# Norms in two groups of columns between grouped weight units of an f32 transformer kernel

## The reference

```python
def rmsnorm(x, g): return x * rsqrt(mean(x * x, axis=-1) + EPS) * g
h = rmsnorm(x, g) * (1 + scale) + shift        # per feature; scale, shift differ for image and context
x = x + gate * (mixer(h) @ w_out)
x = x + gate2 * feed_forward(rmsnorm(x, g2) * (1 + scale2) + shift2)
```

## Time and profile before

| what | value |
|---|---|
| runs | 3505.76, 3510.49, 3510.88 us; median 3510.49 |
| profiled execution | 3510.39 us, span 3509.1 us, mean granted clock 0.984 |
| TensorE busy | 3327.1 us, 95% of the span |
| VectorE busy | 1789.2 us, 51% |
| ScalarE busy | 1255.0 us, 36% |
| GpSimd busy | 233.9 us, 7% |
| DMA | 334.28 MB, mean 95 GB/s |

### The profile page before, as it was taken

The page is one execution under the profiler, slowest core; times in us unless marked ns, Lnnn a source line. Parts: engine busy times, 40 slices in busy tenths (PEclk is TensorE's granted clock), DMA queues, the critical chain, the costliest instruction groups (busy, mean ns, idle before and its releaser), DMA issues.

```text
span 3509.1 us, 43200 instructions
## 1 busy us (share of the span) xinstructions
PE 3327.1 (95%) x18016; PEld 2762.5 (79%) x18016; DVE 1789.2 (51%) x2728; ACT 1255.0 (36%) x1781; POOL 233.9 (7%) x319
## 2 busy tenths in 40 slices
PE   6998989999989999989999999989999989989998
PEld 4787778888877878767888786778888878668886
DVE  3678355333345445547666356366435434644343
ACT  4568342112234234244222435342212243543232
POOL 1001200000110000010001000100000110010001
PEclk9999999999999999999999999999999999999999
DMA  4500133323211211225544211133323221112222
GB/s 195 216 22 1 48 115 126 120 91 126 88 65 54 99 57 60 81 72 172 176 160 147 76 47 55 37 108 126 124 88 127 96 73 66 49 66 99 93 97 90
DMA packets 88643, 334.28 MB, mean 95 GB/s; under 512 B 11264, under 2 KB 14336, under 8 KB 84864
## 3 DMA queue, kind: packets, MB, share of 16 engines
q1 hardware_dynamic: 67280, 252.85, 20.5%
q0 software_dynamic: 21168, 78.65, 7.0%
HBM read 329.37 MB, written 2.10 MB: 94 GB/s over the span
## 4 chain that ended last, share of the span: by engine, by line
PE 90%; ACT 4%; DVE 4%; issue 1%; DMA 0%; POOL 0%; SPq 0%; ACTq 0%; DVEq 0%; POOLq 0%
PE PS L362 65%; PE PS L402 6%; PE PS L387 3%; PE PS L604 3%; PE PS L371 2%; PE PS L582 2%; PE PS L525 1%; PE PS L540 1%; PE PS L697 1%; PE PS L572 1%; PE PS L655 1%; PE PS L513 1%; PE PS L708 1%; ACT aPT L920 1%; ACT WH L768 1%
## 5 line engine op out<-in xcount | busy, mean ns | idle before, releaser
L768 ACT ACTIVATE WH<-WR 128x1024 fp32r<-128x1024 f32 (+1 forms) x376 | 418.8, 1114 | 1499.1 <-PE PS L362 1293.9
L362 PE MATMUL PS<-HH,WH 128*128 128x512 f32 x2912 | 879.9, 356 | 18.5 <-DVE WL L1162 10.0
L362 PE MATMUL PS<-HH,WL 128*128 128x512 f32 x2912 | 876.9, 355 | 0.0
L362 PE MATMUL PS<-HL,WH 128*128 128x512 f32 x2912 | 874.6, 355 | 0.0
L1162 DVE TENSOR_TENSOR WL<-WR,WH 128x1024 fp32r<-128x1024 f32 (+1 forms) x376 | 487.0, 1296 | 751.4 <-ACT WH L768 750.9
L362 PEld LDWEIGHTS PS<-HH,WH 128*128 128x128 f32 x2912 | 481.1, 188 | 109.4 <-issue 14.8
L362 PEld LDWEIGHTS PS<-HH,WL 128*128 128x128 f32 x2912 | 479.5, 188 | 79.6
L362 PEld LDWEIGHTS PS<-HL,WH 128*128 128x128 f32 x2912 | 478.5, 188 | 80.4 <-issue 1.0
L362 PE MATMUL PS<-DH,WL 128*128 128x512 f32 (+1 forms) x1056 | 318.7, 356 | 0.0
L362 PE MATMUL PS<-DH,WH 128*128 128x512 f32 (+1 forms) x1056 | 318.7, 356 | 0.0
L362 PE MATMUL PS<-DL,WH 128*128 128x512 f32 (+1 forms) x1056 | 318.7, 356 | 0.0
(11 more groups left out here) (272 smaller groups left out, 3994.1 us busy)
## 6 DMA issues: line engine op xcount, KB each, us to landing
WR<-in_win SPq DMA_DIRECT2D x176, 512.0 KB, 3.5
AT<-in_adat POOLq DMA_DIRECT2D x144, 512.0 KB, 3.8
WR<-in_wdn SPq DMA_DIRECT2D x64, 704.0 KB, 4.0
WR<-in_wret SPq DMA_DIRECT2D x64, 512.0 KB, 3.2
WR<-in_zin SPq DMA_DIRECT2D x36, 512.0 KB, 3.5
AR<-in_ada SPq DMA_DIRECT2D x8, 1024.0 KB, 11.5
aV<-in_ada SPq DMA_DIRECT2D x8, 1024.0 KB, 4.9
aAR<-in_ada SPq DMA_DIRECT2D x8, 1024.0 KB, 6.6
```

Source lines behind the costliest of these rows:

```text
L362: mm = PE.matmul(dst[:, a:b], w[u % 2][:, k * P:(k + 1) * P], h[:, k, a:b], start=(k == 0 and i == 0), stop=(k == nk - 1 and i == 2))
L768: AC.activation(M.WH[u % 2][:, 0:n], M.WR[u % 2][:, 0:n], COPY).then_inc(*on.up("w_hi", u))
```

## The change

The norms between stages (all but "0a") are made in two groups of columns. For "0b", "1a", "2b" and "3a" group 0 is the image and group 1 the context; for "2a" it is the other way round; for "1b", "3b" and "final" the groups are the two halves of the image. `product_tail` makes the last two units before a norm group by group: group 0 of both, then group 1 of both, with group 0's two mean matmuls inside the first unit's group 1. `product_groups` makes the first two units after it: group 0 in halves of four tiles, then group 1, with group 1's mean matmuls inside the first half. It stands in front of the feed-forwards and of the retention; in front of the mixers of layer 2 the row products go context first, and in front of those of layer 3 they need the image alone.

DVE's `norm` weaves the updates of X, the scaling, the low parts and the two refills of the next stage in one written order, ACT's `norm` does the same with squares, roots and high parts. The scale is now applied by DVE together with the root for every tile (not for tile 0 alone), so that ACT adds the shift and rounds to HH in one instruction; L810 and L814 are gone there. "2a" has no grouped tail: its context comes by DMA early, so its norm is made beside the last product of layer 1. The root, half and scaled tiles have buffers of their own (`NORM`). GpSimd's sums of the tail's tiles, the last norm's scaling and the 8 stores of 128 x 512 are split by group as well (16 stores of 128 x 256). SyncE's waits name group 1.

In the calls, `norm(tag, l, which, segs)` becomes `norm(tag, l, which, update, c)` with c the next stage's first unit, and `mean_square(tag, segs)` is gone but for the first norm. Cut to its core:

```diff
...
+def groups(tag):
+    if tag in ("1b", "3b", "final"):
+        return (0, L, 0), (L, S, 0)
+    return ALL if tag != "2a" else ALL[::-1]
+def tail_tiles(tag):
+    return {"1b": ((4, 5), (6, 7)), "2a": ((), (7,)), "0a": ((), ())}.get(tag, ((6,), (7,)))
+def tail_place(ps, tag, v, g):
+    a, b, _ = groups(tag)[g]
+    return ps[v][:, 512 * g:512 * g + b - a]
...
+    def product_groups(u, dst, tag, between):
+        for g, (a, b, _) in enumerate(groups(tag)):
+            for k0, k1 in ((0, KT // 2), (KT // 2, KT)) if g == 0 else ((0, KT),):
+                for v in range(2):
+                    if g == 0 and k0 == 0:
+                        PE.wait_ge(*on("w_lo", u + v))
+                    for k in range(k0, k1):
+                        between(g, v, k)
+                        if v == 0:
+                            PE.wait_ge(*on("h_lo", (tag, g, k)))
+                        for i, (w, h) in enumerate(((WH, HH), (WH, HL), (WL, HH))):
+                            mm = PE.matmul(dst[v][:, a:b], w[(u + v) % 2][:, k * P:(k + 1) * P], h[:, k, a:b],
+                                           start=(k == 0 and i == 0), stop=(k == KT - 1 and i == 2))
+                    if g == 1:
+                        mm.then_inc(*on.up("product", u + v))
+    def product_tail(u, src, nk, tag, after):
+        hi, lo = src
+        for g, (a, b, _) in enumerate(groups(tag)):
+            for v in range(2):
+                if g == 0:
+                    PE.wait_ge(*on("w_lo", u + v))
+                    PE.wait_ge(*on(*after[v]))
+                for k in range(nk):
+                    beside_tail(tag, g, v, k)
+                    for i, (w, h) in enumerate(((WH, hi), (WH, lo), (WL, hi))):
+                        mm = PE.matmul(tail_place(PS, tag, v, g), w[(u + v) % 2][:, k * P:(k + 1) * P], h[:, k, a:b],
+                                       start=(k == 0 and i == 0), stop=(k == nk - 1 and i == 2))
+                mm.then_inc(*(on.up("product", u + v) if g else on.up("tail", (tag, v))))
+    def mean_part(tag, g, i):
+        a, b, _ = groups(tag)[g]
+        PE.wait_ge(*(on("squared", piece(tag, KT - 1, g)) if i else on("square_summed", piece(tag, KT - 2, g))))
+        mm = PE.matmul(mean_place(PS, tag)[:, a:b], M.ONE[:, :], M.WK[(2, 1)[i]][:, a:b], start=(i == 0), stop=(i == 1))
+        if i == 1:
+            mm.then_inc(*on.up("mean_square", (tag, g)))
+    def beside_tail(tag, g, v, k):
+        if g == 1 and v == 0 and k in (2, 5):
+            mean_part(tag, 0, k // 5)
+    def beside_head(tag):
+        def between(g, v, k):
+            if g == 0 and v == 0 and k in (2, 3):
+                mean_part(tag, 1, k - 2)
+        return between
     def product_pair(u, dst, segs, ready, between=None):
...
                 product(up + 2 * j + 1, PS[1], (HH, HL), KT, segs, free[1])
-            for m in range(KT):
+            for m in range(KT if ch == 0 or l == 1 else KT - 2):
                 after = (None, ("up_taken", (l, (ch + 1) * FC - 1)), (gate, (l, (ch + 1) * FC - 1)))[m] if m < 3 else \
                     ("x_down", (l, ch, m - 2))
-                product(down + m, PS[m % 2 if m else 2], (M.DH, M.DL), FC, segs, after, ("d_lo", l, ch) if m == 0 else None)
+                product(down + m, PS[m % 2 if m else 2], (M.DH, M.DL), FC, segs, after, ("d_lo", l, ch) if m == 0 else None,
+                        context_mean if ch and m == KT - 1 else None)
+        if l != 1:
+            product_tail(down + KT - 2, (M.DH, M.DL), FC, {0: "1a", 2: "3a", 3: "final"}[l],
+                         [("x_down", (l, 1, m)) for m in (KT - 4, KT - 3)])
+    def context_mean(k):
+        if k == 7:
+            for i in range(2):
+                mean_part("2a", 0, i)
...
+        def image_mean(at):
+            if at in (4, 6):
+                mean_part(f"{l}a", 1, at // 6)
+        for g, tiles in enumerate((range(4, 6), range(4)) if l == 2 else (range(4),)):
+            for v in range(2):
+                product_rows(u + v, 4, 4 * v, L, tiles, place, v == 0, v == 1, ("h_lo", f"{l}a", g), True, None,
+                             image_mean if g == 0 and v == 0 else None, l == 3 or g == 1)
         mixed = [PS[3], PS[2]]
         for p in range(ROWS_AT):
             z = MIX[p]
+            if z == 12 and l == 3:
+                PE.wait_ge(*on("h_lo", ("3a", 1, KT - 1)))
             if p == MIXED_AT:
                 PE.wait_ge(*on("av_normed", l))
...
-    def norm(tag, l, which, segs):
-        n = segs[-1][1]
-        if tag == "0a":
-            AC.wait_ge(*on("step", ("scl", 0, 1)))
-        else:
...
-                for a, b, j in segs:
-                    i = AC.activation(HH[:, k, a:b], t[:, a:b], IDENT, bias=MOD[:, l, 24 * which + k, j:j + 1])
-            else:
-                for a, b, j in segs:
-                    i = AC.activation(t[:, a:b], t[:, a:b], IDENT, bias=MOD[:, l, 24 * which + k, j:j + 1],
-                                      scale=M.SCL[:, l, which, k, j:j + 1])
-                i.then_inc(*on.up("h_whole", (tag, k)))
-                AC.wait_ge(*on("h_whole", (tag, k)))
-                i = AC.activation(HH[:, k, 0:n], t[:, 0:n], COPY)
-            i.then_inc(*on.up("h_hi", (tag, k)))
+            AC.wait_ge(*on("h_scaled", ("0a", 0, k)))
...
+    def tail_square(tag, k, g):
+        a, b, _ = groups(tag)[g]
+        AC.wait_ge(*on("square_summed", piece(tag, k - 2, g)))
+        AC.activation(M.WK[k % 2][:, a:b], X[:, k, a:b], SQUARE).then_inc(*on.up("squared", (tag, k, g)))
+    def root(tag, g):
+        a, b, _ = groups(tag)[g]
+        RI, RS, _ = norm_tiles(M, tag)
+        rsqrt((tag, g), RI[:, a:b], mean_place(PS, tag)[:, a:b], RS[:, a:b], ("mean_square", (tag, g)))
+    def high(tag, l, which, g, tiles):
+        a, b, j = groups(tag)[g]
+        for k in tiles:
+            AC.wait_ge(*on("h_scaled", (tag, g, k)))
+            AC.activation(HH[:, k, a:b], norm_tiles(M, tag)[2][(KT * g + k) % 5][:, 0:b - a], IDENT,
+                          bias=MOD[:, l, 24 * which + k, j:j + 1]).then_inc(*on.up("h_hi", (tag, g, k)))
+    def norm(tag, l, which, made, c):
+        first, second = tail_tiles(tag)
+        for v, tiles in enumerate((first, second)):
+            for k in tiles:
+                AC.wait_ge(*on(*made(v, 0)))
+                tail_square(tag, k, 0)
+        root(tag, 0)
+        refill(c)
+        high(tag, l, which, 0, range(1))
+        for k in first:
+            AC.wait_ge(*on(*made(0, 1)))
+            tail_square(tag, k, 1)
+        high(tag, l, which, 0, range(1, 2))
+        refill(c + 1)
+        for k in second:
+            AC.wait_ge(*on(*made(1, 1)))
+            tail_square(tag, k, 1)
+        high(tag, l, which, 0, range(2, 5))
+        root(tag, 1)
+        high(tag, l, which, 0, range(5, KT))
+        high(tag, l, which, 1, range(KT))
+    def norm_context_first(c):
+        tail_square("2a", KT - 1, 0)
+        root("2a", 0)
+        high("2a", 2, 0, 0, range(KT))
+        refill(c + 1)
+        AC.wait_ge(*on("x_down", (1, 1, KT - 1)))
+        tail_square("2a", KT - 1, 1)
+        root("2a", 1)
+        high("2a", 2, 0, 1, range(KT))
...
+    def scaled(tag, l, which, g, k):
+        a, b, j = groups(tag)[g]
+        RI, _, TT = norm_tiles(M, tag)
+        at = KT * g + k
+        if at > 4:
+            VE.wait_ge(*on("h_lo", (tag, (at - 5) // KT, (at - 5) % KT)))
+        VE.scalar_tensor_tensor(TT[at % 5][:, 0:b - a], X[:, k, a:b], SCL[:, l, which, k, j:j + 1], RI[:, a:b],
+                                ALU.mult, ALU.mult).then_inc(*on.up("h_scaled", (tag, g, k)))
+    def low(tag, l, which, g, k):
+        a, b, j = groups(tag)[g]
+        VE.wait_ge(*on("h_hi", (tag, g, k)))
+        VE.scalar_tensor_tensor(HL[:, k, a:b], norm_tiles(M, tag)[2][(KT * g + k) % 5][:, 0:b - a],
+                                MOD[:, l, 24 * which + k, j:j + 1], HH[:, k, a:b].bitcast(F32),
+                                ALU.add, ALU.subtract).then_inc(*on.up("h_lo", (tag, g, k)))
+    def norm(tag, l, which, update, c):
+        at = (tag, l, which)
+        update(0, 0)
+        update(1, 0)
+        root(tag, 0)
+        scaled(*at, 0, 0)
+        update(0, 1)
+        scaled(*at, 0, 1)
+        low(*at, 0, 0)
+        refill(c)
+        scaled(*at, 0, 2)
+        low(*at, 0, 1)
+        update(1, 1)
+        scaled(*at, 0, 3)
+        low(*at, 0, 2)
+        refill(c + 1)
+        for k in range(4, 7):
+            scaled(*at, 0, k)
+            low(*at, 0, k - 1)
+        root(tag, 1)
+        scaled(*at, 0, 7)
+        low(*at, 0, 6)
+        scaled(*at, 1, 0)
+        low(*at, 0, 7)
+        for k in range(1, KT):
+            scaled(*at, 1, k)
+            low(*at, 1, k - 1)
+        low(*at, 1, 7)
...
+    def norm_context_first(c):
+        for g in range(2):
+            if g == 1:
+                down(1, 1, KT - 1, IMG, PS[1])
+                refill(c + 1)
+            root("2a", g)
+            for k in range(KT + 1):
```

(44 more changed lines are left out.)

224 lines of the change are left out of this document (124 added, 100 removed).

## The result

The changed kernel takes 3486.89 us (median of 4 runs, 3484.87 to 3488.96) beside 3510.68 us of the kernel before on the same chip: a ratio of 0.9932, 95% interval 0.9917 to 0.9947, so 23.8 us faster. 3479.5 us was forecast (range 3467 to 3491): the sign and the place were right, a quarter of the gain is missing. A second set on another chip gave 3487.79 beside 3510.93 us, ratio 0.9932 again (0.9920 to 0.9945).

A forecast was written before the change was run, and what follows sets the result against it. TensorE was taken as the bound, with only its waits and low-clock stretches to win. Eight seam gains summed to 32.7 us, less 1.7 for the clock: 3510.5 - 31.0 = 3479.5 us, 8-in-10 range 3467 to 3491.

The forecast's parts named there:

- What bounds the kernel: TensorE is busy 3327.1 of 3509.1 us; only its 182 us of waits, mostly at norm seams, and low-clock stretches can be won.
- part 2: Two column groups at the norm seams: at 0b, B at 45.1 instead of 49.2 us, 4.1 us gained.
- the lists: Engine schedules per seam, from A (last-but-one unit's matmuls start) to B (first matmul behind the next two units): gains sum 32.7 us.
- Part 1: High parts made directly: no time saved by itself in paired seams, but ScalarE is freed; it counts in 3a's row products.
- Prices: Costs per operation: 512-column matmul 0.228 us, 256-column 0.119; 256-wide VectorE operation 0.40; GpSimd add of 256 columns 1.0.
- The last norm: Final norm: DVE's last scale ends 23.5 us after A instead of 26.5, SP 1.1 behind; gain 2.2 us.
- The clock: Low clock behind waits in the heads: uncovered in 1a, 2a and 3b, so 1.7 us off the gain, leaving 31.0.
- Rival (a): Clock stays low through the stutter in seven heads, also at B: 14 us lost, 3493 us; chance 0.11.
- (b): More is hidden in the seams than scheduled, up to 12 us more won: 3466 us; chance 0.08.
- (c): Little is left: ACT and DVE delay the refills, a unit split 4 us late in each head: 3507 us; chance 0.05.
- (d): Weight loads no longer hide behind 888 matmuls of 256 columns: 66.6 us cost, 3546 us; chance 0.03.

The follow-up runs named there:

- run 1: Kernel before, with high parts made directly for every tile of the eight later norms and no groups: 3516.8 us beside 3514.25, ratio 1.0011.
- Run 2: Changed kernel with the high parts made in two steps again, the groups kept: 3509.2 us, ratio 0.9987.
- Run 3: Changed kernel with the two units ahead of the norm multiplied one after the other in 6 seams, norm and head still grouped: 3515.85 us, ratio 1.0002.
- run 11: Changed kernel with the three edits of 10, plus the Silu of CB moved behind the first gate: 3475.21 us, ratio 0.9901.
- run 4: Changed kernel with the third and fourth weight units at 3a made ahead of the context tiles: 3484.48 us, ratio 0.9918.
- 5: Kernel of run 4 with the gated rows' norm (AV) moved behind the second gelu copy in both mixers: 3483.07 us, ratio 0.9921.
- 10: Changed kernel with the edits of 5 (run 4's included), plus 2a's image update, square and weights between the context tiles: 3483.62 us, ratio 0.9924.

## Why the forecast was right in its places and 7 us too good

**What bounds the kernel; part 2; the lists.** Right. All eight seams were forecast within 1.2 us, their sum within 0.3 us of the 31.0 (30.7; 30.9 between the second profiles). At 0b the steps are where the list put them: idle before the pair 2.6 for 3.0, 1.5 us for the weights behind CB's activation, B 44.7 for 45.1 behind A. Only within the pair TensorE idled less, 0.8 and 0.4 for "0.7 + 1.1 + 1.5"; as CB and the weights set the end, that was covered. The signs named beforehand came: the wait of the mean at 2a (3.4 for 3.5), of the weights at 3a (5.8 for "some 6"), VectorE's weight line in place of the low part.

**Part 1.** Right that the direct form saves nothing by itself (run 1) and that it frees ScalarE for the groups; the text didn't say how much hangs on that. Run 2 puts it at 23.1 us of seams. Run 3 puts the order of the two units at 27.3 us; as each takes most of the gain, the two can't be added.

**Prices.** The GpSimd add of 256 columns, taken as 1.0 us, is 1.37; 1b, where it stands on the path, gained 1.7 for 2.4. A 256-wide operation of VectorE costs 0.40 us in a row, as taken.

**The last norm.** 3.0 for 2.2, though the list held. The end in the timeline of the kernel after (the last eight of the 16 stores):

```profile
3481.92 3.26 DVE L1468 SCALAR_TENSOR_TENSOR X<-X,FG,nRI 128x256 f32<-128x256 f32 x8
3482.44 3.78 SPq L2129 DMA_DIRECT2D out_x<-X  x8
```

VectorE's last scale ends 23.3 us after A (of 23.5), SP needs 0.47 us a store, as taken, and ends 1.0 us behind it (of 1.1). Most of the rest is behind the last issue, where the program ended 1.5 us later instead of 1.9; the stores are half as large now.

**The clock: the step that failed.** "I take off 1.7 for these: 31.0" counts what a lower clock costs within the heads and takes the stretches between seams as fixed. Within the seams the low level lasted 71 and 75 us in the two profiles before and 40 and 34 after. That the sum came out at 30.7 beside 31.0 doesn't show the 1.7: "2a" and "3b", where a slow PE was to be uncovered, keep their length with more or less of it (3b 33.51 us with 6.8 or 3.4 us at the low level in the changed kernel and 33.50 with none in run 11; 2a 35.15 with 6.8 us, and the same with 3.4 in run 4). So in part the sum is luck: errors of up to 1.2 us in single seams cancel. Between them (the opening aside) it didn't stay put: 27 and 41 us in two profiles of the kernel before, 47 and 46 in two of the changed one. By length, means of two profiles each, stretch 2a-2b lost 1.9 us and 3a-3b 3.3, 1a-1b 1.0; about 6 us in all. Seams 30.8 (mean of two) minus 6 is 25, where the medians show 23.8 and 23.1; the pace of the products, 3.4 us that an execution has or hasn't in stretch 2b-3a, is more than the difference. The opening, ahead of the first seam, moves too: 422.6 and 422.8 us before, both with 17.1 us of low clock, 421.3 and 425.3 after, with 20.5 and 37.6. Rival (a) had the right agent, low clock in places that had none, and mostly the wrong place: the heads got better (0.96 for 0.90 at 0b), what lies behind them worse. At 3a it had the place too: "at B too, where nothing covers it".

**Why the clock is low for longer between the seams of the changed kernel** is settled for one part only. At 3a it is the new wait: in all seven profiles of kernels that have it (5.6 to 7.6 us) the clock stays low for 3.0 to 5.9 us from B on, in the four in which its cause is taken away (runs 4, 5, 10, 11) for 2.0 us once and not at all in the others. The rest is open. The waits there are the same to 0.6 us. In 2a-2b a wait of 1.27 us stands in both kernels, 92.5 us behind B; a low clock follows it in eight of the eleven profiles of kernels with groups (not in runs 2, 10 and 11) and in none of the three without. Over all stretches but the opening the low level lasts 27 to 41 us in the three profiles without groups and 36 to 52 in the eleven with them: a tendency, not a gap. That fits a clock that depends on when a wait falls and not only on how long it is, but no run varied that alone.

**Rivals (b), (c), (d).** (b) overstated what hides; (c) little left: the refills were late only where the lists had them late. (d) is refuted: the groups' matmuls of 256 columns run at 0.119 us, each with its own load. By the rule of the Trainium skill ("TensorE: Matmul & The Clock Gate", section "The mechanism") that a load overlaps running matmuls only when it goes to another row group, they would take 0.21 us, the estimate of the prediction. The trace disagrees here as it did before the change.

## What to carry to other kernels

When two engines alternate on a chain ahead of a third, cut it in pieces only if the producer works by the same pieces and no link needs two passes: here, without the one or the other, a ninth or a quarter of the gain in the seams was left. Sum a forecast by seams, but keep an allowance for the stretches between them: their waits stay the same while the clock behind the waits doesn't, and a new long wait at a seam's end is paid again behind it. After such a change, read the new waits for work of a later stage that is queued ahead of what is needed next (a table load, the parts for columns that nobody reads yet); moving four such pieces gave another 12.6 us, clock and pace of the products included.

## What the runs showed of the hardware

- Plain products of 512 and 256 columns run at one of two paces, 0.353 or 0.347 us a pair (units of 8.48 or 8.32 us), the slower for the first 20 units of a stretch, some 170 us, with TensorE busy throughout and the granted clock at 1.00 in both (568 and 579 products in 100 us). The same kernel has the one or the other in different executions: in 2b-3a six of fourteen profiles had the slow one, in layer 0's first such stretch all but one. What sets it is open.
- Two profiled executions of one unchanged kernel differ by 9.2 us in span (3509.1 and 3518.3): 4.2 us in 2b-3a by pace and clock, 2.6 us in the last feed-forward stretch (336.4 and 339.0), where 5.6 us ran at the lower clock, the rest in smaller pieces of the same kind. One profile is no ground for naming a cause under 5 us.
- Removing a wait of 5.8 us gained 4.7 us in its seam, took away the low clock right behind it, and uncovered another wait of 4.1 us on another engine's queue.
- GpSimd's add of 128 rows takes 1.37 us for 256 columns, 1.76 for 512 and 2.23 for 768 (means in the changed kernel).
